# A hybrid SSD/RG-LRU/expert step on one core: opening rebuilt, exp/tanh gate, expert weights in 32 KB runs

## The reference

```
xn = RMSNorm(x);  proj = xn @ w_in -> z | xBC | dt | gate_y | x_lru | g_m | g_r
SSD branch   : conv4+silu(xBC), dt = softplus, chunked state space scan, RMSNorm(y * silu(z))
RG-LRU branch: xl = conv4(x_lru); r, i = sigmoid(block matmuls of xl)
               log_a = -8 r softplus(-lambda); a = exp(log_a)
               u = sqrt(-expm1(2 log_a)) * (i * xl);  h_t = a_t h_(t-1) + u_t
x += (sigmoid(g_m) * (ssd @ w_out_m) + sigmoid(g_r) * ((h * gelu(gate_y)) @ w_out_r)) @ w_o
x += HierMoE(RMSNorm(x))      top 1 of 4 groups, top 2 of its 8 experts, 32 experts
     expert(t) = (silu(t @ w_gate[e]) * (t @ w_up[e])) @ w_down[e],  2048 -> 512 -> 2048
x += sigmoid(RMSNorm(x) @ w_ple_gate) * (p @ w_ple);   y = RMSNorm_final(x)
```

## Time and profile before

| | |
|---|---|
| median of 3 runs | 3201.22 us (3198.62 to 3201.91) |
| profiled execution, its own time | 3202.14 us |
| its span | 3200.6 us |
| TensorE busy | 2893.5 us, 90% |
| VectorE, ScalarE, GpSimd busy | 573.3, 362.9, 51.5 us |
| moved by DMA | 646.69 MB |
| granted TensorE clock, mean | 0.963 of 2.4 GHz |

### The profile page before, as it was taken

One profiled execution on the slowest core, in us unless ns is written; L12 is line 12 of the kernel. 1 busy time (PEld: TensorE's weight loads), 2 busy tenths in 40 slices (PEclk: granted clock), 3 DMA queues, 4 the chain that ended last, 5 costly groups with the idle time before them and its releaser, 6 DMA issues.

```text
span 3200.6 us, 33844 instructions
## 1 busy us (share of the span) xinstructions
PE 2893.5 (90%) x14016; PEld 1868.9 (58%) x14016; DVE 573.3 (18%) x1102; ACT 362.9 (11%) x633; POOL 51.5 (2%) x78
## 2 busy tenths in 40 slices
PE   3989899999999999999999988888888888887697
PEld 2556565555555555555557865555455555554586
DVE  2333324324433100000000020000000000010311
ACT  2121211212222000000001020000000000000101
POOL 1000000000000000000000000000000000000000
PEclk9999998999999999999999999999999999999799
DMA  6351533323232333332228229999999999998422
GB/s 131 96 158 59 164 105 116 117 86 111 85 111 79 105 105 105 105 104 94 93 76 276 96 103 398 401 392 402 394 401 399 395 401 398 402 396 313 142 79 92
DMA packets 359596, 646.69 MB, mean 202 GB/s; under 512 B 7788, under 2 KB 196708, under 8 KB 340260
## 3 DMA queue, kind: packets, MB, share of 16 engines
q1 hardware_dynamic: 340944, 600.06, 52.5%
q0 software_dynamic: 6528, 27.54, 3.2%
q10 hardware_dynamic: 12090, 18.62, 1.6%
HBM read 616.16 MB, written 30.04 MB: 202 GB/s over the span
## 4 chain that ended last, share of the span: by engine, by line
PE 79%; DMA 15%; DVE 4%; issue 1%; ACT 1%; ACTq 0%; POOL 0%; DVEq 0%; POOLq 0%; SPq 0%
PE bank L1278 21%; PE bank L1177 13%; DMA arena<-in_w_exp_up_dram 12%; PE bank L1378 11%; PE bank L1248 8%; PE bank L1357 6%; PE bank L1317 5%; PE bank L1412 5%; PE bank L1396 4%; DVE arena L920 1%; PE bank L1232 1%; DMA arena<-in_conv_r_w_dram 1%; PE bank L1414 1%; DMA arena<-in_state_ssm_dram 1%; PE bank L1142 1%
## 5 line engine op out<-in xcount | busy, mean ns | idle before, releaser
L1278 PE MATMUL bank<-arena 128*128 128x384 f32 x2048 | 660.6, 486 | 0.0
L1378 PE MATMUL bank<-arena 128*64 128x256 f32 x4096 | 487.7, 401 | 108.2 <-DMA arena<-in_w_exp_up_dram 65.9
L1278 PEld LDWEIGHTS bank<-arena 128*128 128x128 f32 x2048 | 389.3, 190 | 271.2
L1378 PEld LDWEIGHTS bank<-arena 128*64 128x64 f32 x4096 | 312.4, 145 | 293.7 <-DMA arena<-in_w_exp_up_dram 73.1
L1177 PE MATMUL bank<-arena 128*128 128x384 f32 x1280 | 416.4, 488 | 0.0
L1177 PEld LDWEIGHTS bank<-arena 128*128 128x128 f32 x1280 | 244.0, 191 | 170.0 <-issue 3.5
L1248 PE MATMUL bank<-arena 128*128 128x384 f32 x1024 | 331.7, 487 | 3.0 <-ACT arena L586 3.0
L1248 PEld LDWEIGHTS bank<-arena 128*128 128x128 f32 x1024 | 194.4, 190 | 139.9 <-ACT arena L586 4.9
L1396 PE MATMUL bank<-arena 128*64 128x512 f32 x1024 | 231.7, 606 | 30.0 <-DVE arena L1082 23.8
L1357 PE MATMUL bank<-arena 128*128 128x128 f32 x1632 | 188.2, 277 | 2.5 <-DVEq L1032 2.5
L1357 PEld LDWEIGHTS bank<-arena 128*128 128x128 f32 x1632 | 185.0, 193 | 8.7 <-issue 8.7
(11 more groups left out here) (303 smaller groups left out, 1354.4 us busy)
## 6 DMA issues: line engine op xcount, KB each, us to landing
arena<-in_w_exp_gate_dram SPq DMA_DIRECT2D x32, 4096.0 KB, 20.1
arena<-in_w_exp_up_dram SPq DMA_DIRECT2D x32, 4096.0 KB, 23.3
arena<-in_w_exp_down_dram SPq DMA_DIRECT2D x32, 4096.0 KB, 18.9
arena<-in_w_in_dram SPq DMA_DIRECT2D x48, 2048.0 KB, 8.3
arena<-in_w_out_m_dram SPq DMA_DIRECT2D x8, 2048.0 KB, 8.1
arena<-in_w_out_r_dram SPq DMA_DIRECT2D x8, 2048.0 KB, 8.2
arena<-in_w_o_dram SPq DMA_DIRECT2D x8, 2048.0 KB, 8.2
expert_rows<-arena ACTq DMA_DIRECT2D x64, 256.0 KB, 6.9
```

The source lines that it names most:

```text
L1278: last = mm(banks[2 * s + cc][:, 0:T], slab[s % 2][:, k, cc * 128:(cc + 1) * 128], rhs[:, k, :], start=(k == 0), stop=(k == KC - 1))
L1378: last = mm(banks[2 * x + i][h * SLOTS:(h + 1) * SLOTS, 0:FF // 2], xe[:, k, x * SLOTS:(x + 1) * SLOTS], w[:, k, h * (FF // 2):(h + 1) * ( ...
```

## The change

**Opening.** SyncE first loads `g_mix` alone (after the first memset), then x and `w_dt`, and no longer waits for `params_in` before the slabs. GpSimd issues the three history loads ahead of most constants. ScalarE loads the Sqrt table at once, squares the x tiles, and only then issues the 12 other parameter loads. TensorE transposes `g_mix` alone, norms, transposes the histories, runs dt's 16 matmuls on four column groups (partial sums in 4 x 32 rows), transposes `prow`, and one matmul with `sel` adds the four parts. `dt_columns` runs behind the first slab of the first SSD group.

**SSD.** The first group is peeled off the loop on TensorE and VectorE. In all groups the decay subtraction comes after the six convolutions.

**Gate.** 1 - a^2 = -(1 + a^2) tanh(log_a): a square of `lr = a` and one fused step replace three steps with the reciprocal.

**Experts.** Partition p now reads rows 16p to 16p+15 of gate and up (one run of 32 KB), and for each half of down two neighbouring rows (16 KB). `xtok` and `hrow` are written in the permuted order, so that the matmuls read them as before; the gains come from `gffn_p`, loaded in that order.

```diff
 sync:
+            sp.wait_ge(consts_ready, 1)
+            sp.dma_start(prow[0:16, 0, :], a["g_mix"].rearrange("o (c p) -> (o c) p", p=128)).then_inc(gmix_in, 16)
...
-            sp.wait_ge(params_in, 16 * PARAM_DMAS)
...
-                sp.dma_start(dst, a[name][0, ds(e, 1), :, :].rearrange("o (k p) c -> p (o k) c", p=128)).then_inc(ew_loaded[i], 16)
+                w = a[name][0, ds(e, 1), :, :]
+                if i < 2:
+                    w = w.rearrange("o (p k) c -> p (o k) c", p=128)
+                else:
+                    w = w.rearrange("o (h p c) d -> p (o h) c d", h=2, p=128)
+                    dst = dst.rearrange("p (h c) d -> p h c d", h=2)
+                sp.dma_start(dst, w).then_inc(ew_loaded[i], 16)
 gpsimd (moved up from behind the constants, own semaphore hist_in):
+            pool.dma_start(hist_rows[:, 0:XBC], a["state_ssm_conv"][0].rearrange("b k c -> (b k) c")).then_inc(hist_in, 16)
+            pool.dma_start(hist_rows[:, XBC:XBC + D], a["state_lru_conv"][0].rearrange("b k c -> (b k) c")).then_inc(hist_in, 16)
+            pool.dma_start(sm[:, 0:128], a["state_lru"][0].rearrange("b (c p) -> (b c) p", p=128)).then_inc(hist_in, 16)
...
+            pool.dma_start(gffn_p, a["g_ffn"][0].rearrange("(p k) -> p k", k=KC)).then_inc(gffn_in, 16)
 scalar:
+            act.wait_ge(consts_ready, 3)
+            A(sm[:, 250:251], ones[:, 0:1], ACT.Sqrt)
+            for t in range(NT):
+                act.wait_ge(x_loaded[t], 16)
+                square_tile(t, x_in[:, t, :])
             (then the parameter loads; the copies of the histories now stand before the dt steps)
...
-                A(lr, la_, ACT.Exp)
+                A(lr, la_, ACT.Exp).then_inc(l_ex, 1)
-                A(la_, lt, ACT.Sqrt).then_inc(l_s, 1)
+                A(la_, lt, ACT.Sqrt, scale=-1.0).then_inc(l_s, 1)
...
-                A(xtok[t], x_res[:, t, :], ACT.Identity, scale=rstd3[:, t:t + 1]).then_inc(xtok_ready, 1)
+                A(v3(xtok[t], KC), x_res[:, t, :].rearrange("p (m k) -> p k m", k=KC), ACT.Identity,
+                  scale=rstd3[:, t:t + 1]).then_inc(xtok_ready, 1)
-                        A(hrow[x], banks[2 * x][:, 0:FF // 2], ACT.Silu).then_inc(gu_act, 1)
+                        A(v3(hrow[x], 2), banks[2 * x][:, 0:FF // 2].rearrange("p (m c) -> p c m", c=2), ACT.Silu).then_inc(gu_act, 1)
 vector:
-            link(V.tensor_copy(pcol, banks[6][:, 0:384]))
+            link(V.tensor_copy(pcol[:, 0:16], banks[6][:, 0:16]))
...
+            link(TT(sel, ident[:, 0:32], ident[:, 32:64], ALU.add))
+            link(TT(sel, sel, ident[:, 64:96], ALU.add))
+            TT(sel, sel, ident[:, 96:128], ALU.add).then_inc(dt_sel, 1)
+            dve.wait_ge(dt_part, 1)
+            V.tensor_copy(dt4, banks[4][:, 0:T]).then_inc(dt_sel, 1)
+            dve.wait_ge(ptr_done, 2)
+            link(V.tensor_copy(pcol, banks[2][:, 0:384]))
...
+            def ssd_group(g):
+                for m in range(6):        # the six convolutions, now first
+                    ...
+                    if m == 3 and isinstance(g, int):
+                        dve.wait_ge(dt_tr, 1)
+                        V.tensor_copy(tokcol, v3(banks[5][:, 0:320], 10)).then_inc(tok_ready, 1)
+                dve.wait_ge(tok_ready, 1)
                 dve.wait_ge(cum_loaded, 48 * g + 48)
                 (the three subtractions and the minimum, then as before)
+            ssd_group(0)
+            with dve.Fori(1, GROUPS) as g:
+                ssd_group(g)
...
-                link(TS(la_, lt, -1.0, 1.0, ALU.mult, ALU.add))
-                link(V.reciprocal(la_, la_))
-                STT(lt, lt, -2.0, la_, ALU.mult, ALU.mult).then_inc(l_w, 1)
+                dve.wait_ge(l_ex, g + 1)
+                link(TT(xl, lr, lr, ALU.mult))
+                dve.wait_ge(l_at, g + 1)
+                STT(lt, xl, 1.0, lt, ALU.add, ALU.mult).then_inc(l_w, 1)
 tensor:
-            pe.wait_ge(params_in, 16 * PARAM_DMAS)
-            for b in range(3):
-                last = tr(banks[6][:, 128 * b:128 * b + 128], prow[:, b, :], ident)
+            pe.wait_ge(gmix_in, 16)
+            tr(banks[6][:, 0:16], prow[0:16, 0, :], ident[0:16, 0:16]).then_inc(ptr_done, 1)
...
+            pe.wait_ge(hist_in, 16 * 3)     (history transposes, then)
+            pe.wait_ge(dt_loaded, 16)
+            for k in range(KC // 4):
+                for j in range(4):
+                    last = mm(banks[4][32 * j:32 * j + HEADS, 0:T], w_dt[:, 4 * k + j, :], xnT[:, 4 * k + j, :],
+                              start=(k == 0), stop=(k == KC // 4 - 1))
+            last.then_inc(dt_part, 1)
+            pe.wait_ge(params_in, 16 * PARAM_DMAS)
+            for b in range(3):
+                last = tr(banks[2][:, 128 * b:128 * b + 128], prow[:, b, :], ident)
+            last.then_inc(ptr_done, 1)
+            pe.wait_ge(dt_sel, 2)
+            mm(banks[5][0:HEADS, 0:T], sel, dt4, start=True, stop=True).then_inc(dt_done, 1)
...
                 group_slab(0, slab[2])
+                if isinstance(g, int):
+                    pe.wait_ge(hist_evac, 3)
+                    dt_columns()
```

More of the change, by code:

```diff
@@ L3 @@
 from contextlib import ExitStack
-PARAM_DMAS, CONSTS = 13, 14
-SSD_LINKS, LRU_LINKS = 50, 24
+PARAM_DMAS, CONSTS = 12, 14
+SSD_LINKS, LRU_LINKS = 50, 23
 D = 2048
@@ L205, in hybrid_stream_step @@
         rrow = rr.take(16)
+        gffn_p = rr.take(KC)
         npass_i = rr.take(2).bitcast(i32)
@@ L556, in _ @@
                 square_tile(t, x_in[:, t, :])
-            act.wait_ge(consts_ready, CONSTS)
-            act.wait_ge(setup_in, 16 * 7)
+            for name, at in (("g_ffn", P_GFFN), ("g_ple", P_GPLE), ("g_ssm", P_GSSM),
+                             ("b_lru_a", P_BA), ("b_lru_x", P_BX), ("lru_lambda", P_LAM)):
+                rows(r16(a[name]), at, 16)
+            rows(r16(a["conv_m_b"]), P_CB, 24)
+            rows(r16(a["conv_r_b"]), P_CB + 24, 16)
+            rows(a["conv_m_w"].rearrange("o k (c p) -> (o k c) p", p=128), P_CW, 96)
+            rows(a["conv_r_w"].rearrange("o k (c p) -> (o k c) p", p=128), P_CR, 64)
+            assert n == PARAM_DMAS, n
+            act.wait_ge(consts_ready, CONSTS)
+            for b in range(2):
+                act.wait_ge(hist_T, b + 1)
+                A(convmem[:, 20 * b:20 * b + 20, HIST:27], v3(banks[6 + b][:, 0:480], 20), ACT.Copy).then_inc(hist_evac, 1)
+            act.wait_ge(hist_T, 3)
+            A(lru_h0, v3(banks[3][:, 0:128], NSEQ), ACT.Copy).then_inc(hist_evac, 1)
+            act.wait_ge(setup_in, 16 * 4)
             act.wait_ge(dt_step, 1)
@@ L901, in _ @@
                     link(TT(ss_acc, ss_acc, ysq[j % 2], ALU.add))
-                link.end(GROUPS, SSD_LINKS)
+                assert link.k == SSD_LINKS, link.k
+            ssd_group(0)
+            with dve.Fori(1, GROUPS) as g:
+                ssd_group(g)
+            link.base, link.k = ssd_at + GROUPS * SSD_LINKS, 0
             dve.wait_ge(hn_stored, 16 * KC)
@@ L1032, in _ @@
             dve.sem_inc(xe_evac, 2)
+            dve.wait_ge(gffn_in, 16)
             xe_columns(0, 0)
@@ L1130, in _ @@
             pe.wait_ge(consts_ready, CONSTS)
-            pe.wait_ge(params_in, 16 * PARAM_DMAS)
-            for b in range(3):
-                last = tr(banks[6][:, 128 * b:128 * b + 128], prow[:, b, :], ident)
-            last.then_inc(ptr_done, 1)
+            pe.wait_ge(gmix_in, 16)
+            tr(banks[6][:, 0:16], prow[0:16, 0, :], ident[0:16, 0:16]).then_inc(ptr_done, 1)
             def norm_T(n):
@@ L1146, in _ @@
                 norm_T(t)
-            pe.wait_ge(n_evac, 12 + 4)
-            pe.wait_ge(dt_loaded, 16)
-            for k in range(KC):
-                last = mm(banks[4][0:HEADS, 0:T], w_dt[:, k, :], xnT[:, k, :], start=(k == 0), stop=(k == KC - 1))
-            last.then_inc(dt_done, 1)
-            pe.wait_ge(setup_in, 16 * 7)
+            pe.wait_ge(hist_in, 16 * 3)
             for b in range(2):
@@ L1166, in dt_columns, with ssd_group @@
                 last.then_inc(dt_tr, 1)
-            dt_columns()
-            pe.wait_ge(hist_evac, 3)
-            with pe.Fori(0, GROUPS) as g:
+            def ssd_group(g):
                 def group_slab(m, w):
@@ L1198, in _ @@
                 last.then_inc(aux_done, 1)
+                pe.wait_ge(tok_ready, 1)
                 for t in range(NT):
@@ L1238, in _ @@
                     last.then_inc(st_mm, 1)
+            ssd_group(0)
+            with pe.Fori(1, GROUPS) as g:
+                ssd_group(g)
             with pe.Fori(0, GROUPS) as g:
```

37 lines of the change are left out of this document (16 added, 21 removed).

## The result

The changed kernel takes 3107.18 us (median of 4 runs, 3104.95 to 3108.33) against 3200.44 us (4 runs, 3198.62 to 3201.91). The ratio is 0.9708, with a 95% interval of 0.9691 to 0.9725: 93 us faster. The prediction was 3088 us in a range of 3064 to 3126. So the sign and the range hold, and 19 us less came than forecast. 3107 also lies outside the band of the forecast proper (3070 to 3105), in that of rival 2 (3105 to 3126).

The account below looks back on a forecast made before the run. DMA, with TensorE close behind, was taken to bound the experts; in the opening TensorE waits. From 3202.14 us, experts -75, opening -36, gate -3 and token tiles +1 gave 3089, as median 3088 us; range 3064 to 3126.

Parts of the forecast that it names:

- rival 2: TensorE starves weight queue by late down loads, 16 to 24 us, or x_sample is late: 3105 to 3126; chance 0.14.
- the law from two rates of the earlier trace: Expert weight loads: 10.4 ns per run plus 0.0364 ns per byte; 436 GB/s at 32 KB, 30.3 us per expert.
- 2.4 us each, -75 us: Expert stage: longer weight runs save 2.4 us per expert over 31 experts, bounds 62 to 83 us.
- the tight point: Odd expert's down buffer: TensorE needs 26.3 us until the next down load, the queue holds 30.3; 4 us left.
- I take 43: Opening: projection stream starts at 43 us, between 41.5 (nothing late) and 49.5 (x_sample behind d_skip); -36 us.
- Gate -3: Exp/tanh gate: a product and one fused step replace three VectorE steps; -3 us, bounds 0 and -3.
- moved decay work 0: VectorE's subtractions and minimum after the convolutions, 8 us at most, fit in 17.24 us of idle time; cost 0.
- token tiles +1: ScalarE writes three token tiles from a read with a step of 16 elements; twice the time costs 2 us; +1 taken.
- (1) slow long runs: Expert weights: each engine sits in one stretch of memory, 320 GB/s, 41 us an expert, near 3410; chance 0.04.
- (3) Little gain from the runs: Expert weights: long runs are cut up again or gain few per cent, stage gain 0 to 30, 3134 to 3164; chance 0.08.
- (4) All waits gone: Expert stage: TensorE's DMA waits go wholly (-107), near 3057 us; chance 0.04.
- The signs named: Expert windows at 425 to 435 GB/s, far fewer packets, gate/up waits some 40 us, pairs 61 us, d_skip late as now.

Follow-up runs that it names:

- Run 1: The changed kernel with the old weight, token, activation and gain layouts (2 KB runs for gate and up, 8 KB for down): 3165.28 us, ratio 0.9896.
- Run 7: The changed kernel with the token picking of a pair moved behind the odd expert's down matmuls: 3097.51 us, ratio 0.9672.
- run 3: The changed kernel with the three history loads put back behind the constants, ahead of d_skip: 3099.73 us (one run).
- run 9: The kernel before with the exp/tanh gate alone: 3198.42 us against 3200.94, ratio 0.9992.
- run 8: The changed kernel with the token tiles read in order and written with a step of 128 elements: 3104.51 us (one run).

## Why the prediction came out as it did

- **That DMA bounds the experts and longer runs raise its rate: right, and shown.** Run 1 takes the whole stage gain away, and the law from two rates of the earlier trace rows, 432 GB/s for an expert's mix, is met by 434 in full windows. The section of the Trainium skill weighed there, "DMA: Bandwidth & Descriptors", "Why small descriptors are slow (HBM only)", allowed 2 KB runs a gain of 4.5% at most, by the estimate from its overhead per packet. Windows of this case show 387 against 434, 12%, so the measurement decides.
- **The stage's gain: the term that was mis-sized.** "2.4 us each, -75 us" measured (1048.6 - 988.3) / 31 = 1.95 us each, -60.3, just below the lower bound of 62. The step that failed: 30.3 and 31.0 us per expert were worked out with a queue that is always full. The prediction saw the tight point ("4 us are left", 1.1 with slow matmuls) and made a rival of it, at 1 to 1.5 us a pair, but left it out of the sum. It happened in each of the three pairs looked at: 385, 388 and 360 GB/s over 15 us in place of 434 are 1.7, 1.6 and 2.6 us. Over the 900 us of the stage the mean is 422 in place of 434, and 2.8% of 988 us is 27 us. The stage is longer than the law's 23 + 31 x 30.3 = 962 by 26. So the mean rate accounts for the whole shortfall against the law. (26 is more than the 15 us missed: the choice of 2.4 in place of 2.7 had taken off 9, and before the change the same sum was 3 short.) That the queue runs thin at the late load is read from the trace. Run 7 bears on it only in part: it moved the hole from down to gate and shortened pairs by 0.5 us. No run kept the queue full all the time, so how much of the 26 us a kernel without late loads would get back was not measured. Nor was the share of the small stores, whose landing went from 6.9 to 13.2 us; no run took them out.
- **The opening: the stream's start 37 us earlier forecast (80.17 to 43), 30.4 measured.** The chain of steps was good on both sides: 41.5 if nothing is late against 42.38 (run 3), 49.5 behind `d_skip` against 49.80. The step that failed is the choice between: "I take 43", nearer the good end, when both the later x and the earlier histories spoke for the bad one. Of the inner terms, the dt projection took 4.39 us (3.2 to 6.4 were given), and history transposes 2.97.
- **Gate -3, moved decay work 0, token tiles +1:** with the 1.3 for the dt transposes the prediction had -0.7 between stream and experts; it measured -3.4. The gate fits at -3, though only by the profile (run 9). The token tiles took 11.01 us in place of 5.78, the case of "twice the time", and the wait grew from 2.48 to 3.95, +1.5. The ten dt transposes inside the stream take 0.7 to 0.8 us, not 1.3. The note cited there, of the Trainium skill's "SBUF — State Buffer", section "Door 1: The DMA port swizzle", calls a step of 4 fp32 elements (16 B) free and charges longer ones; here a step of 4 costs as much as one of 16 (run 8). That leaves -2.6 of the -3.4, which the prediction did not have at all. It lies in the projection matmuls: those of the SSD stage took 416.4 us before and 414.5 now, those of the LRU stage 331.7 and 330.9 (330.9 in run 9 too, so that part goes with the gate). For the first the granted clock says why. Before, the stream began just behind an idle time of 10.41 us, at a mean clock of 0.54, so mostly at the level of 1.2 GHz; now TensorE has been busy since 37.22, and it begins at 1.00. (In run 3, where TensorE waited 2.54 us just ahead, it is 0.55.)

```profile
80.17:85.00 4.83, 4.83 (x9) 2.71 (x9) 2.24 (x8) 0.60 (x2) 1.79 (x2) 0.54 0.73 214
```

```profile
49.80:55.00 5.20, 5.20 (x17) 3.15 (x17) 1.50 (x3) 3.71 (x6) 0.00 (x0) 1.00 0.85 269
```

- **The rivals.** (1) slow long runs: refuted, 434 GB/s. (2) Starved queue and late `x_sample`: both came about, each of which alone made the rival, and 3107 is in its band. 0.14 was too little; nothing in the trace of before had put its two conditions far off. (3) Little gain from the runs: no. (4) All waits gone: no, 65.3 us of gate and up waits stayed, where 40 had been forecast.

- **The signs named.** `d_skip` lands as late as before (14.9 and 23.9 us after its issue). Packets fell to 228561. The full windows are at the law's rate, but not every window is. A pair takes 61.8 us on average (926.8 us for 15), and 62.1 without the first, not 61.

In sum: the experts gave 15 us less and the opening 7 us less than forecast, and the small terms nearly 3 more: 19.

## What to carry to other kernels

Before a rate measured in a full window is multiplied out over a stage, write down when each load is issued and how long the queue lives without it; if the slack is a few microseconds, a faster transfer will use it up, and the starved case is the forecast. To move the late load's last reader forward helps only if no other buffer then comes free late in its place. And when an edit moves work over the end of the stretch that you measure, compare a period of the loop, not the stretch. In an opening look first for small loads with scattered elements, and issue them last or read them as whole rows: that was worth 15 us in the kernel before, for 8 KB. An edit that moves loads forward is priced by what they are moved ahead of.

## What the hardware showed unexpectedly

- Two loads of 4 KB each, gathered element by element and broadcast to 64 partitions, landed after 14.9 and 23.9 us and held back 1 MB of x and 256 KB of weights issued 4 us ahead of them by 17 us. Read as one row and broadcast to 128 partitions the same values landed in 7.2 us.
- The rate goes on rising at long runs: with full queues 387 GB/s at 2 KB, 423 at 8 KB (windows of 10 us), 434 at 16 and 32 KB (50 us). Over 900 us of the stage the kernels with 2 KB (down 8 KB), 8 KB and 32 KB (down 16 KB) keep up 398, 412 and 422.
- A changed order of elements costs the same whether the step is on the read or the write side of ScalarE's copy (11.01 and 10.83 us against 5.78), and at a step of 4 elements (11.57) as at 16.
- Beside longer packets of the weights the 256 KB stores take longer to land: 6.9 us before, 9.2 with 8 KB runs, 13.2 after.
- A stream of matmuls that began after 10.41 us of idle TensorE ran its first 4.8 us at a granted clock of 0.54; begun right behind other matmuls it had 1.00.
